# A fifth 2 MB place for expert weights, in the half of the head tile that holds the tokens' rows until they are stored

## What is computed

```python
h2 = rms_norm(x, norm2_gain)                       # 512 x 1024
combine_w = ...                                    # 512 x 16: two experts of one group per token
a = einsum('nd,edf->nef', h2, w_gate)              # w_gate, w_up: 16 x 1024 x 512
u = einsum('nd,edf->nef', h2, w_up)
hid = silu(a) * u * combine_w[:, :, None]
x = x + einsum('nef,efd->nd', hid, w_down)         # w_down: 16 x 512 x 1024
```

## Time and profile before

| | us |
|---|---|
| median of 3 runs | 1919.01 |
| the three runs | 1923.16, 1919.01, 1918.89 |
| profiled execution, its own time | 1922.02 |
| span of the profiled execution | 1920.2 |
| mean granted TensorE clock of it | 0.978 |

### The profile page before, as it was taken

The page is one execution under the profiler, slowest core; times in us unless marked ns, Lnnn a source line. Parts: engine busy times, 40 slices in busy tenths (PEclk is TensorE's granted clock), DMA queues, the critical chain, the costliest instruction groups (busy, mean ns, idle before and its releaser), DMA issues.

```text
span 1920.2 us, 27569 instructions
## 1 busy us (share of the span) xinstructions
PE 1813.5 (94%) x11244; PEld 1538.0 (80%) x11244; DVE 1179.7 (61%) x1702; ACT 887.8 (46%) x1443; POOL 331.0 (17%) x223
## 2 busy tenths in 40 slices
PE   6999999999999999999999999989989969999993
PEld 6988788999998788999999766755568758777772
DVE  5565544554375544454774688587654356878786
ACT  5425443324334434334343455356633246676762
POOL 3332222001333222001000374300010010000001
PEclk9999999999999999999999999999989979999997
DMA  6212101223212211222222200203242348999994
GB/s 179 72 56 75 51 23 59 96 67 110 91 56 72 67 43 46 92 92 93 89 89 88 66 23 23 88 32 100 69 162 88 130 166 318 380 379 385 377 371 165
DMA packets 156103, 241.44 MB, mean 126 GB/s; under 512 B 9593, under 2 KB 101018, under 8 KB 155978
## 3 DMA queue, kind: packets, MB, share of 16 engines
q1 hardware_dynamic: 148602, 212.88, 32.7%
q0 software_dynamic: 4464, 16.25, 2.2%
q10 hardware_dynamic: 2912, 10.55, 1.4%
HBM read 223.41 MB, written 16.25 MB: 125 GB/s over the span
## 4 chain that ended last, share of the span: by engine, by line
PE 78%; DVE 13%; ACT 5%; issue 2%; DMA 1%; POOL 1%; SPq 0%; ACTq 0%; POOLq 0%; DVEq 0%
PE acc L842 31%; PE acc L1339 10%; PE acc L1084 8%; PE acc L1109 7%; PE acc L951 4%; PE acc L1015 3%; DVE ring_split L2810 2%; PE acc L992 2%; PE acc L1173 2%; PE acc L1187 1%; PE acc L1204 1%; PE acc L859 1%; PE acc L1003 1%; DVE hres_split L2810 1%; DVE v L2510 1%
## 5 line engine op out<-in xcount | busy, mean ns | idle before, releaser
L842 PE MATMUL acc<-h_split,ring_split 128*128 128x264 f32 x1088 | 308.4, 283 | 0.0
L842 PEld LDWEIGHTS acc<-h_split,ring_split 128*128 128x128 f32 x1088 | 204.3, 188 | 0.0
L842 PE MATMUL acc<-h_split,qk_split 128*128 128x264 f32 x384 | 109.7, 286 | 0.0
L842 PE MATMUL acc<-ring_split,qk_split 128*128 128x264 f32 x384 | 108.7, 283 | 0.0
L1109 PE MATMUL acc<-ring_split,h_split 128*128 128x256 f32 x384 | 107.9, 281 | 0.0
L842 PE MATMUL acc<-h_split,krope_split 128*128 128x264 f32 x320 | 94.0, 294 | 3.8 <-ACT latent L1688 2.4
L842 PE MATMUL acc<-ring_split,krope_split 128*128 128x264 f32 x320 | 90.8, 284 | 0.0
L2159 DVE TENSOR_TENSOR ring_split<-ring,o_split 128x1024 fp32r<-128x1024 f32 (+1 forms) x32 | 44.9, 1418 | 72.5 <-ACT o_split L1499 72.4
L3088 POOL DMA_INDIRECT latent<-h_rows,rows_of x16 | 18.4, 1148 | 387.7 <-PE acc L1325 230.1
L1339 PE MATMUL acc<-qk_split,krope_split 128*128 128x512 f32 x240 | 75.8, 397 | 8.5 <-DVE ring_split L2810 6.2
L2964 POOL TENSOR_TENSOR latent<-latent 128x528 f32<-128x528 f32 x18 | 26.8, 1491 | 313.2 <-ACT latent L1494 312.8
(11 more groups left out here) (575 smaller groups left out, 5828.8 us busy)
## 6 DMA issues: line engine op xcount, KB each, us to landing
ring<-in_w_in SPq DMA_DIRECT2D x64, 1024.0 KB, 5.2
ring<-in_w_expert_gate SPq DMA_DIRECT2D x13, 2048.0 KB, 10.3
ring<-in_w_expert_up SPq DMA_DIRECT2D x12, 2048.0 KB, 11.2
ring<-in_w_expert_down SPq DMA_DIRECT2D x11, 2048.0 KB, 11.7
ring<-in_w_out SPq DMA_DIRECT2D x12, 1024.0 KB, 5.1
hres<-in_w_expert_down SPq DMA_DIRECT2D x5, 2048.0 KB, 10.4
hres<-in_w_expert_up SPq DMA_DIRECT2D x4, 2048.0 KB, 10.8
y_rows<-gate ACTq DMA_DIRECT2D x16, 512.0 KB, 7.2
```

What stands on the lines that cost most here:

```text
L842: ins = nc.tensor.matmul(dst[0:rows_, half, 0:HALF], w[:, k, :], x[:, c], start=(k == 0 and i == 0), stop=(k == last and i == 2), skip_gro ...
```

## The change

`RAW` becomes 5 and the places gain one: the lower half of the head tile. Granule i then lies in place i mod 5 in place of i mod 4, and waits for the product of granule i-5 in place of i-4. Granule 4 (down 0), the first in the new place, waits until the four stores of `h_tok` have landed (`h_stored` at 64), where before it waited for the product of gate 0. One semaphore more counts the loads of the new place. No instruction on PE, ACT, DVE or POOL is added or taken away, and the same 48 loads are issued by SP in the same order.

```diff
-        RAW, UPS, HALF_W = 4, 6, SLOT_F // 2
-        raw = [ring[:, i * SLOT_F:(i + 1) * SLOT_F] for i in (2, 0, 1)] + [hres[:, :, :].rearrange("p c t -> p (c t)")[:, 0:SLOT_F]]
+        RAW, UPS, HALF_W = 5, 6, SLOT_F // 2
+        raw = [ring[:, i * SLOT_F:(i + 1) * SLOT_F] for i in (2, 0, 1)] + [hres[:, :, :].rearrange("p c t -> p (c t)")[:, 0:SLOT_F],
+                                                                              qkf[:, 0:SLOT_F]]
         raw_low = [ring_split[:, i * SLOT_F:(i + 1) * SLOT_F] for i in (2, 0, 1)] \
-            + [hres_split[:, :, :].rearrange("p c t -> p (c t)")[:, 0:SLOT_F]]
+            + [x[:, :, :].rearrange("p c t -> p (c t)")[:, 0:SLOT_F] for x in (hres_split, qk_split)]
...
                 elif slot < SLOTS:
                     sp.wait_ge(psum_filled, at(psum_filled, (("gl", DC - 1), ("out2", 5), ("out2", DC - 1))[slot]))
-                else:
+                elif slot == SLOTS:
                     sp.wait_ge(psum_filled, at(psum_filled, ("x_tok", QT - 1)))
                     sp.wait_ge(dve_made, at(dve_made, ("h3", DC - 1)))
+                else:
+                    sp.wait_ge(h_stored, 16 * QT)
                 sp.dma_start(raw[slot].rearrange("p (k m) -> p k m", k=DC if kind != "down" else HID // P),
```

## The result

| | before | after |
|---|---|---|
| median of 20 runs, us | 1922.51 | 1925.35 |
| lowest and highest, us | 1918.78, 1925.69 | 1922.36, 1932.44 |
| span of the profiled execution, us | 1920.2 | 1921.0 |

The ratio after to before is 1.0020, 95% interval 1.0011 to 1.0028: slower by 3.8 us (2.1 to 5.4), by the medians 2.8. That is inside the 0.3% that the prediction calls "same", but the time lies above its range, 1917.0 to 1924.0. The first three runs of before had a median of 1919.01; with twenty it is 1922.51, so 3.5 us of the 4.9 us between 1920.5 and 1925.35 are the level from which the sum started. The rest, 1.3 us, is the sum: +1.5 us were forecast and +2.8 us came, by the medians.

What follows compares the result with a forecast made beforehand. PE was taken to be held by its own work and a loop with ACT and DVE, not by weight loads. Terms: 0 for ACT's waits, 0 for stores and later gathers, +1.5 for the first gather; 1919.0 + 1.5 = 1920.5 us, range 1917.0 to 1924.0.

Steps and rivals of the forecast that it cites:

- The level, 1919.0: Whole kernel: median of the runs shown, 3.0 us below the profiled 1922.0, taken as the base of the forecast.
- The clock, half a microsecond off the delay: Gate 0, PE's clock rising from half to full: a 2.0 us later start costs 1.0 to 2.0, taken as 1.5.
- The size of the gather's delay, 2.0 us: First token gather beside early down 0: 1.2 us for the bytes plus most of a 1.1 us tail.
- the sign: Profile after: the first gather should land 7 to 8 us after its issue in place of 5.28.
- The upper bound, +4.4: First gather delayed like the fourth, landing at 1582.2; as a rival with the clock following, 1923.4 us, chance 0.08.
- The early load's place and mechanism: Start of experts: down 0 issued near 1567, not 1590.21, delays the first gather, passed in full to the first gate product.
- Places, 0 us: Expert stage: the fifth place removes ACT's 7.4 us of weight waits, hidden in its pause for PE; gain 0.
- Depth in flight, stores and later gathers, 0 us: Expert stage steady state: bytes in flight do not rise, result stores keep 12 us of room; cost 0.
- The rival in which a full SP queue holds back ACT: Expert stage: stalled SP issue also slows ACT's result stores, up to 3.0 us in 15 periods, 1964 us; chance 0.06.
- Taking turns: First gather: DMA engines alternate queues packet by packet, so it runs at half rate, through near 1578.9, 1.1 us late.
- the fourth gather: Later token gather, issued 1.1 us behind a single weight load, landed after 8.3 us; basis of the upper bound.
- The first rival: Expert stage: late weights do reach PE, so the fifth place returns 7.4 us, 1911.6 us; chance 0.07.

Runs made afterwards that it cites:

- idle load: Kernel before, four places, plus an early 2 MB load of down 0's weights that nobody reads, issued when the tokens' rows are stored: ratio 1.0023.
- three places: Kernel before with `RAW` 3 in place of 4, so each granule lands one product later: ratio 1.0216.
- the faster loop: Kernel before with ScalarE's copy and store of the result of e-1 behind both upper parts of down e: 0.9922; same order with five places: 0.9917.
- the copy behind both parts and up 1 ahead: Changed kernel with ScalarE's result copy behind both upper parts of down e and up 1 loaded ahead of the `h_tok` stores: 0.9907, again 0.9903.
- down 0 behind gate 0: Changed kernel, five places, but down 0 loaded only when gate 0's product is done, as in the kernel before: ratio 1.0009.

## Why the prediction was right or wrong

**The level, 1919.0: wrong, and this is the step that failed.** The profiled execution of before, 1922.0, gave 1923.5 for the changed kernel. The forecast then took 3.0 us off, to get down to the median of three runs. Two of these three are among the five lowest of twenty (1918.78 to 1920.11; the other fifteen lie at 1921.34 and above), and the median of the twenty is 1922.51. This term is 3.5 us too low, out of a miss of 4.9 us. The range was built on the same three runs and ended at 1924.0, less than 1 us above the highest of them. The cause of the spread is only partly known: in the 18 profiles the router starts anywhere between 1558.08 and 1569.54 us, so much of it comes from stages ahead of the change.

**The clock, half a microsecond off the delay: wrong, and this is the term of the change that failed.** "Between 1.0 and 2.0 I take 1.5" supposed that the rise either stays or follows the start, so that the end of gate 0 would be late by at most the delay. With the router at half clock, the kind of execution that the prediction had read, the rise moved 3.6 us for a start that was 2.3 us later, and the end came 2.9 us later: the clock took 0.6 us and gave nothing back. With the router at full clock it stayed and gave back 1.2 of 2.5 us. The step's result, +1.5 us, lies between the two ends that were measured, +1.3 and +2.9, and the medians gave +2.8.

**The size of the gather's delay, 2.0 us: nearly right.** Like for like it is 2.3 us with the router at half clock and 2.5 us at full clock. With the idle load the gather landed 20.15 us behind the router's start, which is 1580.05 on the profile of before, where the end of all bytes and most of a tail gave 1579.8. What the prediction did not see is the second kind of execution, in which up 1 also delays the gather, before and after; there the gather took 8.8 us, more than the 7 to 8 us given as the sign. The upper bound, +4.4, held in both.

**The early load's place and mechanism: right.** Issued at 1566.90 (about 1567 said), DMA engines busy through, the first gather late and passed on in full to gate 0's start. The idle load shows it without the fifth place.

**Places, 0 us: right.** Periods, ACT's waits and its pause came out as written (no wait for weights, 4.67 us of pause at 1659.41 where 4.5 was said), five places without the early load beside the gather measured 1.0001, the rest of 281.5 us is the same with four and five, and three places showed how large the room was.

**Depth in flight, stores and later gathers, 0 us: right.** ACT's stores took 0.34 to 0.38 us to issue. The rival in which a full SP queue holds back ACT has nothing to stand on in the trace; it was not provoked by a run of its own.

**Taking turns.** By the rule that the prediction took from the Trainium skill ("DMA: Bandwidth & Descriptors", section on queues, rings and completion order), taking turns packet by packet, it estimated that the gather would be 1.1 us late. The traces show more, as the fourth gather had: 2.3 and 2.5 us for the 2 MB of down 0.

**The first rival**, late weights that reach PE, was wrong for this kernel and is right for the one with the faster loop, where the fifth place takes 3.3 to 4.2 us off the rest.

## What to carry to other kernels

One more buffer is worth only what its loads' lateness exceeds the pause of the engine that waits for them; read the pause beside the wait, and look at the length of the period with and without it, before you look at the DMA share. A transfer that is moved into an idle stretch of the DMA engines has to be checked against whatever small transfer the chain waits for there; if it must go early, put it where it is over in time. A delay is to be read between two executions of the same kind, and against a kernel that has all the other transfers of the kernel before: here a pair that looked like twins gave 3.5 us where 2.4 to 2.5 were right, because one of them had moved a second load away. And the level of a forecast wants more than three runs, when two of three can lie 3 us below the median of twenty.

## What the runs showed of the hardware

At a DMA share of 1.02 and 379 GB/s, the same before and after, the loads were not the bound (1700 to 1800 us). With the faster loop the same engines moved 399 GB/s with four places and 403 GB/s with five. The full share told nothing of the room left.

A gather of 128 rows of 4 KB from GpSimd took 5.2 to 5.4 us from issue to landing in nine profiled executions in which no load was left to move when its own rows came; 6.4 to 6.9 us in four with the end of a load of the SP queue beside it, and 7.55 to 8.94 us in five in which 2 MB and more were still to move.

The moment at which PE's granted clock falls from the 2.4 GHz to the 1.2 GHz level in the router part differs between executions of the same program: the router's 20 matmuls took 4.42 us in one profile and 2.38 us in another of the kernel with five places, the copy behind both parts and up 1 ahead. It moves the issue of the first gather by 2.6 us and the start of gate 0 only by 1.1 us in that kernel and by 1.5 us in kernels that are like before up to there (22.38 against 20.87 in the table), because the earlier gather meets more of a load.

The rise back to the 2.4 GHz level does not keep its distance from the start of the product it falls into: it came 3.3 us behind gate 0's start in the profile after, 4.7 us before, 5.9 us with down 0 behind gate 0 and 6.0 us with the idle load.
